# A transformer block with product-key experts: ScalarE makes one gate row in four, the row dots are dealt out anew, and the strips begin four chunks later

## The reference, cut to what matters

```
q = (h @ w_q).reshape(t, 8 heads, 2, 128)          # h: normed tokens
s = einsum('thpc,hpnc->thpn', q, subkeys)          # 2 x 128 keys per head
sv, si = top_k(s, 16)                              # per half
cand_s = sv[..., 0, :, None] + sv[..., 1, None, :] # 16 x 16 pairs
top_s, top_pos = top_k(cand_s, 16)                 # 16 experts per head
expert = i * 128 + j                               # of 16384
gate = softmax(top_s)
act = gelu(einsum('thkd,td->thk', u[expert], h))
out = einsum('thk,thkd->td', gate * act, v[expert])
```

## Time and profile before

| | |
|---|---|
| median of 3 runs | 3011.3 us (3008.99 to 3013.48) |
| profiled execution | 3013.73 us, of which the span 3011.9 |
| PE busy | 2864.3 us (95%), 17261 matmuls |
| DVE busy | 1946.2 us (65%) |
| ACT busy | 786.6 us (26%) |
| POOL busy | 1586.8 us (53%) |
| moved by DMA | 763.56 MB, 254 GB/s over the span |
| mean granted TensorE clock | 0.978 |

### The profile page before, as it was taken

The page is one execution under the profiler, slowest core; times in us unless marked ns, Lnnn a source line. Parts: engine busy times, 40 slices in busy tenths (PEclk is TensorE's granted clock), DMA queues, the critical chain, the costliest instruction groups (busy, mean ns, idle before and its releaser), DMA issues.

```text
span 3011.9 us, 45791 instructions
## 1 busy us (share of the span) xinstructions
PE 2864.3 (95%) x17261; PEld 2436.7 (81%) x17261; DVE 1946.2 (65%) x4600; ACT 786.6 (26%) x1426; POOL 1586.8 (53%) x1088
## 2 busy tenths in 40 slices
PE   7999989999999999999999869899999999999998
PEld 6878758899999999999999868666677677666765
DVE  5011263599888999899999665445566555555664
ACT  3222242222222222333333212212222222222222
POOL 1111020246566677655555667566666656566662
PEclk8999989999999999999999989999999999999999
DMA  3100012235777777789998999799999999999996
GB/s 133 42 29 29 15 50 113 105 109 199 268 264 265 264 262 262 264 321 328 324 330 321 363 398 353 256 328 320 327 316 332 338 336 335 330 322 319 322 325 226
DMA packets 300379, 763.56 MB, mean 254 GB/s; under 512 B 21456, under 2 KB 136528, under 8 KB 297424
## 3 DMA queue, kind: packets, MB, share of 16 engines
q0 software_dynamic: 110592, 402.70, 37.6%
q1 hardware_dynamic: 189648, 359.13, 33.4%
HBM read 669.47 MB, written 92.27 MB: 253 GB/s over the span
## 4 chain that ended last, share of the span: by engine, by line
PE 82%; DVE 8%; DMA 4%; POOL 3%; issue 2%; ACT 1%; SPq 0%; DVEq 0%; ACTq 0%; POOLq 0%
PE bank L1770 29%; PE bank L1437 27%; PE wide L1790 6%; PE bank L1734 5%; PE bank L1482 3%; PE bank L1646 3%; PE bank L1663 2%; DMA w_raw<-in_u 2%; PE bank L1503 1%; PE bank L1504 1%; PE bank L1505 1%; PE wide L1555 1%; DVE u_row L1261 1%; DVE eq L1248 1%; POOL u_row L580 1%
## 5 line engine op out<-in xcount | busy, mean ns | idle before, releaser
L1437 PE MATMUL bank<-h_hi,w_hi 128*128 128x320 f32 (+1 forms) x2400 | 578.5, 322 | 51.0 <-POOL w_lo L571 48.3
L631 POOL DMA_INDIRECT v_row<-in_v,ids_t x384 | 381.8, 994 | 389.7 <-PE wide L1790 281.9
L1437 PE MATMUL bank<-h_lo,w_hi 128*128 128x320 f32 (+1 forms) x2400 | 559.7, 315 | 0.0
L1437 PE MATMUL bank<-h_hi,w_lo 128*128 128x320 f32 (+1 forms) x2400 | 559.7, 315 | 0.0
L571 POOL TENSOR_TENSOR w_lo<-w_raw,w_hi 128x1024 fp32r<-128x1024 f32 x144 | 363.2, 2522 | 366.4 <-ACT w_hi L855 354.0
L1354 DVE TENSOR_TENSOR a_lo<-prod,a_hi 128x384 fp32r<-128x384 f32 (+1 forms) x256 | 258.0, 1008 | 444.1 <-ACT a_hi L921 428.0
L1261 DVE CUSTOM_DVE_ANT_0 u_row<-wide,u_row 128x1024 f32<-128x1024 f32 x384 | 454.2, 1221 | 83.1 <-DMA u_row<-in_u_rows,ids 76.2
L580 POOL DMA_INDIRECT u_row<-in_u_rows,ids x384 | 432.4, 1126 | 106.4 <-issue 76.6
L1437 PEld LDWEIGHTS bank<-h_hi,w_hi 128*128 128x128 f32 x2400 | 402.8, 191 | 60.2 <-issue 30.2
L1770 PE MATMUL bank<-v_hi,a_hi 128*128 128x512 f32 x1272 | 407.3, 401 | 10.4 <-POOL v_lo L620 5.3
L1437 PEld LDWEIGHTS bank<-h_lo,w_hi 128*128 128x128 f32 x2400 | 409.2, 190 | 4.0
(11 more groups left out here) (205 smaller groups left out, 3624.0 us busy)
## 6 DMA issues: line engine op xcount, KB each, us to landing
w_raw<-in_u SPq DMA_DIRECT2D x128, 512.0 KB
v_raw<-in_v SPq DMA_DIRECT2D x32, 2048.0 KB
act_d<-act_st SPq DMA_DIRECT2D x128, 320.0 KB
g_d<-g_st SPq DMA_DIRECT2D x20, 2048.0 KB
a_raw<-act_d SPq DMA_DIRECT2D x32, 768.0 KB
g_raw<-g_d SPq DMA_DIRECT2D x32, 768.0 KB
w_raw<-in_w_q SPq DMA_DIRECT2D x32, 512.0 KB
a_raw<-act_d SPq DMA_DIRECT2D x32, 512.0 KB
```

Source lines behind the costliest of these rows:

```text
L631: nc.gpsimd.indirect_dma_start(v_row[k % RING][:, :], None, v_rows, bass.IndirectOffsetOnAxis(ids_t[:, t, TW * s + c:TW * s + c + 1], 0)). ...
L1437: ins = pe.matmul(banks[h][:, 0:n], lhs[:, part], rhs[:, k, h * n:(h + 1) * n], start=(k == 0 and lhs is lhs_hi and rhs is h_hi), stop=(k ...
```

## The change

Three things are changed together.

1. In the strips, VectorE writes three of the four `gate_j` rows of a group. The fourth is made by ScalarE in two activations: (j - iota) squared, into `off_j`, then Relu(gate - gate x that square), which is the gate where iota equals j and 0 elsewhere. It needs the negated gates (`gate_n`, two new VectorE instructions) and a wait on itself. `last_gate` is called for groups 0 and 1 ahead of the loop, then for m + 2 behind each eviction `to_strip(m)`. TensorE waits for `gk_done` too.
2. `ROWS_TILE` goes from 14 to 18 and `ROWS_PAIR` from 13 to 16: 178 rows are used ahead of the strips (158 before), 160 in them (130), 46 behind them (96).
3. `B0` goes from 40 to 42 and `EXP_BODY` from 37 to 39: the strips begin with chunk 84 of the row of items instead of 80; 20 chunks are left behind them instead of 24.

```diff
-EXP_BODY = 37
-B0 = 40
+EXP_BODY = 39
+B0 = 42
-ROWS_TILE = 14
+ROWS_TILE = 18
-ROWS_PAIR = 13
+ROWS_PAIR = 16
...
+        gate_n = at("gate_n", 193.5, [P, DS])
+        off_j = at("off_j", 196, [P, 2, P])
...
+            def last_gate(m):
+
+                t = 4 * m + 3
+                nc.scalar.activation(off_j[:, m % 2, :], iota[:, :], ACT.Square, scale=-1.0,
+                                     bias=route_t[:, 1, t:t + 1]).then_inc(off_done, 1)
+                act.wait_ge(off_done, m + 1)
+                nc.scalar.activation(gate_j[:, m % 2, 3, :], off_j[:, m % 2, :], ACT.Relu,
+                                     scale=gate_n[:, t:t + 1], bias=route_t[:, 2, t:t + 1]).then_inc(gk_done, 1)
+
+            act.wait_ge(rt_ev, 8)
+            for m in range(2):
+                last_gate(m)
             for n in range(4 * PAIRS):
-                for m in range(4):
-                    to_strip(4 * n + m)
+                for m in range(4 * n, 4 * n + 4):
+                    to_strip(m)
+                    if m + 2 < 16 * PAIRS:
+                        last_gate(m + 2)
                 chunk(B0 + n // 2, n % 2)
...
             dve.wait_ge(rt_ev, 6)
+            for hf in range(2):
+                cols = slice(hf * WA, hf * WA + half_width(hf))
+                V.tensor_scalar(gate_n[:, cols], route_t[:, 2, cols], -1.0, None, ALU.mult).then_inc(rt_ev, 1)
...
-                for k in range(4):
+                for k in range(3):
                     ins = V.tensor_scalar(gate_j[:, m % 2, k, :], iota[:, :], route_t[:, 1, t + k:t + k + 1],
                                           route_t[:, 2, t + k:t + k + 1], ALU.is_equal, ALU.mult)
                 ins.then_inc(gj_done, 1)
...
                 pe.wait_ge(oh_done, it * 16 + (8 * s2 + n + 1))
                 pe.wait_ge(gj_done, it * 16 + (8 * s2 + n + 1))
+                pe.wait_ge(gk_done, it * 16 + (8 * s2 + n + 1))
```

More of the change, by code:

```diff
@@ L312, in build @@
         gj_done = sem("gj_done")
+        off_done = sem("off_done")
+        gk_done = sem("gk_done")
         gp_done = sem("gp_done")
```

## The result

| | before | after |
|---|---|---|
| median (20 runs each) | 3011.2 us | 3018.2 us |
| profiled execution | 3013.7 us | 3015.4 us |
| VectorE busy | 1946.2 us | 1907.9 us |
| ScalarE busy | 786.6 us | 901.8 us |

The ratio is 1.0022, 95% interval 1.0015 to 1.0029: the kernel became 6.9 us slower, where -4 us was forecast. One of the changed kernel's twenty executions took 14210 us at a granted clock of 0.186 and is left out of the ratio. One profiled execution each shows only 1.6 of the 6.9 us.

The account below looks back on a forecast made before the run. TensorE, busy 95% of the span, was taken to bound the kernel, so only holes or added work there count. Strips +18, front +4 and behind the strips -26 summed to -4 us, about 3007 us, range 2994 to 3021.

Parts of the forecast that it names:

- Gathers' traffic: Strips: about 345 GB/s fits; rows asked for 7 to 8 us ahead are late now and then, 0 to 8 us, taken as 1.5.
- The strips, step by step: Strips: costs of rows, one-hots, ScalarE's activations, TensorE's extra wait and gathers, summing to +18 us.
- the sum without late rows: Strips: the predicted sum of +18 us less its 1.5 us term for late rows, +16.5.
- rival C: Strips: rows come late and the chain takes the whole wait; at 0.5 us a turn +16, 3027 us; chance 0.12.
- 40 d: Strips: the cost if a dot waits d us once in each turn; d = 0.1 cancels the gain.
- against: Strips, objection to rival C: 2 MB stores come only every second chunk; 9.6 us of lead leaves turns without row waits.
- The turn's arithmetic: Strips: a four-dot turn of 11.87 us less two one-hots of 0.255 gives 11.36 in all 40 chunks, +15 us.
- Cover 2.6 us: price nothing: Strips: ScalarE's 0.9 us per group is done near 4.9 us, TensorE needs it at 7.5; cost nothing, uncovered 36 us.
- The front: Ahead of the strips: GpSimd's extra gathers delay w_lo; +2 at the first tile, +2 at later tiles, bounds +1 to +9.
- Behind the strips: Tail: first ten chunks unchanged at 93 us, remaining ten lose all gathers, 71 us; -26 us, bounds -28 and -8.
- rival E: Strips: Square not resident with GELU, so table loads cost up to 20 us; +16, 3027 us; chance 0.03.
- rival B: Tail gives more as its first ten chunks relax, or strips cost less, turns near 11; 2996 or 2985 us; chance 0.27.

Follow-up runs that it names:

- e12: Changed kernel with ScalarE's gate row of group 4n+5 behind the GELUs and w_hi, and rows asked for eight ahead: 3008.5 us, ratio 0.9998.
- e13: Changed kernel with each strip's gates stored as two 1 MB transfers, the second one chunk later: 3010.1 us, ratio 1.0001.
- c_after_again: The changed kernel unaltered, run again for a second profiled execution: 3020.7 us.
- e2: Kernel before with the new constants (18 and 16 rows, later strips), all gate rows on VectorE: 3025.6 us, ratio 1.0053.
- e1: Changed kernel with the old constants, so only ScalarE's gate rows differ from the kernel before: 3010.8 us, ratio 1.0002.
- e5: Changed kernel with ScalarE making the gate row of group 4n+5 behind the chunk's GELUs and w_hi: 3009.9 us, ratio 1.0006.
- e6: Kernel of e5 with three of a chunk's four dots behind group 4n+1 and one behind 4n+3: 2989.4 us, ratio 0.9929.
- e7: Kernel of e2 with three dots behind group 4n+1 and one behind 4n+3: 2997.6 us, ratio 0.9965.
- e9: Changed kernel with rows asked for eight ahead in the strips instead of five: 3013.9 us, ratio 1.0015.
- e8: Changed kernel, ScalarE's order kept, with three dots behind group 4n+1 and one behind 4n+3: 3002.4 us, ratio 0.9973.
- e3: Changed kernel with a chunk's four dots dealt out as two behind group 4n+1 and two behind 4n+3: 2998.4 us, ratio 0.9962.
- e10: Kernel of e6 with rows asked for eight ahead in the strips: 2993.5 us, ratio 0.9939.

## Why the prediction was wrong

- **The step that failed** is "Gathers' traffic" in "The strips, step by step": "Rows will be late now and then: 0 to 8 us, taken as 1.5." It had the lead nearly right (8.2 to 8.7 us measured, "about 7 to 8 us" said), but held it against a row's 7.4 us from one place and took the average rate, 345 GB/s, as fitting. Beside a 2 MB store a row took 8.3 us in the median over the strips, otherwise 5.5. The chain to the third group was 7.75, 7.85 and 7.81 us in the mean of 38 turns where a turn without a late row has 7.51: 9 to 13 us, less 1.5 for VectorE's copy of the next tile (L1284). So late rows took 8 to 12 us, and the fourth group's delay 5, 0 and 2: together 12 to 13 us where the sum had 1.5 + 1. e12 (rows early, ScalarE reordered) and e13 (store split) bring the strips to 458.5 and 459.2, that is +16 and +16.5, where the sum without late rows said +16.5.
- **This is rival C**, in every second turn, to which only a chance of 0.12 was given. By its "40 d", with 0.2 to 0.3 us in the mean of all turns, the time is -4 + 8 to 12 = +4 to +8; measured +7. That close a match is partly luck, since other terms moved too: between the forecast's terms and the measured ones lie 7 us in the strips, 3 behind them and 1 in the front. Its "against", that stores come only every second chunk, was the mechanism itself, and the turns cited for it had three dots and 8.9 to 9.4 us of lead by their rows, not 9.6.
- **The turn's arithmetic held.** 11.36 predicted; 11.33 in c_after_again, the chain 7.51 in the regular turns of all three, e2's turns 11.84. One dot 1.17, one gate row 0.255 us.
- **"Cover 2.6 us: price nothing"** for ScalarE's delay was true for TensorE. That it was true for VectorE in this kernel is luck of the place: w_lo now ends at 5.56 us in the turn and is_i of 4n+2 begins at 5.96. "GpSimd's w_lo follows w_hi 0.9 us later, with a whole chunk of time left" missed two effects: w_lo 0.5 us later also blocks VectorE where is_i meets it (e1: the whole gain gone), and the rows are asked for 0.5 us later (e5, which takes that back, is 5 us faster by the ratios).
- **The front**, +4 with bounds 1 to 9: +5, and both halves are seen. From item 42 on, the changed kernel is behind by 1.5, 2.6 and 2.6 us at item 56 (predicted +2 for the first tile); the rest comes with the later tiles.
- **Behind the strips**, -26 with bounds -28 and -8: -23. The first ten chunks were unchanged, as predicted: 94.8 us before, 94.3, 95.0 and 95.0 after, by the GELUs' starts; their waits for w_raw stayed (the first two rows here). The other ten took 73.9, 73.6 and 75.4 us, 3 over their matmuls instead of 2 (the third row is just ahead of them). The rest of the difference is that the other fourteen took 125.8 us before, counted in this way, where the prediction's stretch had 127:

```profile
1755.58 1.06 ACT L859 ACTIVATE w_hi<-w_raw 128x1024 fp32r<-128x1024 f32 x1 [11.25 <-DMA w_raw<-in_u]
...
1795.43 1.06 ACT L859 ACTIVATE w_hi<-w_raw 128x1024 fp32r<-128x1024 f32 x1 [11.16 <-DMA w_raw<-in_u]
...
1831.19 1.06 ACT L859 ACTIVATE w_hi<-w_raw 128x1024 fp32r<-128x1024 f32 x1 [6.72 <-DMA w_raw<-in_u]
```

- **The table load** (rival E) did not come, and rival B fell with the tail. In the strips B was half right in principle: with w_lo out of the way and the dots not in one block, ScalarE's gate rows bring turns down to 10.59 us (e6) from 11.08 (e7).
- **Open**: why the fourth group's matmuls end 0.1 to 0.25 us late in some executions (in nearly all turns of e9's and e13's profiles, in none of c_after_again's, with the same order of work). Why the chain to the third group is 7.60 us in e5 and e12, not 7.51. And e9's median lies 6 us above its own profile, so its worth in the strips is not fully seen in the timed runs.

## What to carry to other kernels

A row's lead has to be held against its latency beside the largest transfer that runs at the same time, not against the average rate; splitting that transfer in time was here worth at least as much as asking earlier (e13 against e9). When work is taken off one engine and given to another, follow what the second engine does later, too: here the move's price lay on a third engine, whose instruction slid into the way of the first, and whose requests went out later. A block of work placed at one point of a chain costs its whole length; dealt out over two of the places where the engine waits anyway, the same work cost 26 us less (e2 to e7).

## What the runs showed of the hardware

- **A VectorE tensor_tensor from SBUF stands still while GpSimd runs a tensor_tensor that began before it.** is_i takes 0.69 us alone, 1.28 (e8), 1.29 (e1), 2.19 (e3) and 2.66 us (e10) beside w_lo. It met a running w_lo about 200 times in the eighteen profiles and each time ended 0.54 to 0.64 us behind it, while w_lo kept its 2.4 us. The Trainium skill (GPSIMD Engine Reference, Specifications) says that the SBUF interfaces are shared and that VectorE's instructions with two SBUF inputs contend; the runs agree, and here it is VectorE that waits, nearly the whole overlap. It is not always the one that loses: beside VectorE's two-input passes in the front a w_lo took 3.96 us. The row dots beside w_lo stay at 1.22 us. One of their two inputs, `wide`, lies in PSUM, which fits the same sentence; no run moved it to see.
- **A 2 MB store raises the latency of row gathers by half.** In c_after_again rows took 8.3 us from issue to landing beside it and 5.5 without (medians of 76 and 72 rows); the DMA engines' share was 0.92 on the average.
- **Square runs beside GELU without a table load**, 0.396 us for 128 columns, 160 times.
